# Prologue of a two-branch encoder layer: whole rows of norm weights, one scaling instruction per tile, two parameter queues, and the Newton step of four tiles on GpSimd

## Chip, cores and metric

One core of a Trainium2 chip runs the kernel. The metric is the device time of one execution in microseconds (us); lower is better. Matmul and weight load run on TensorE (PE in the profile), elementwise work on VectorE (DVE), activations and copies on ScalarE (ACT), further elementwise work on GpSimd (POOL); SP issues most of the loads.

## What is computed

```python
x = concat(x_prompt (1024 rows), x_sample (64 rows))        # 1088 x 2048, float32
h = x * rsqrt(mean(x*x, axis=-1) + EPS) * g                  # g = norm_gain, 2048
u, z_ssm, q, k, v, z_att, f = split(h @ w_in)                # 2048 x 6152
# S5 branch: dt = exp(log_dt); abar = exp(a_re*dt) * (cos(a_im*dt), sin(a_im*dt))
y_ssm, state = s5_scan(u, ...);  y_ssm = rmsnorm(glu(gelu(y_ssm)) * silu(z_ssm))
# attention branch: per-head rmsnorm of q, k; causal attention with forget gates
y_att = rmsnorm(attention(q, k, v, logf) * silu(z_att))
y = x + concat(y_ssm, y_att) @ w_out
```

One layer, float32 in and out. The prompt rows begin a stream; the 64 sample rows continue one with 128 cached rows. The outputs are y, the new cache rows and the final S5 states.

## The kernel before

**The whole.** Each float32 operand is split into a high part (rounded to the matmul's float32r type) and a low part (the remainder), and a product is three matmuls: high by high, high by low, low by high. The normalised input, transposed to features by tokens, stays on chip in two arrays, `XH` and `XL`. A prologue builds them; then come eight turns of the S5 branch (`body` of `state_space`), the attention heads, and the output projection. Nothing of the prologue runs again.

**The prologue.** It takes x in nine tiles (`TT` = 9; 128 rows each, the last has 64). For tile m:

- SP loads it (`ld_x[m]`). Tiles 2, 3 and 6 land in columns of `XHF`/`XLF` that are not yet in use (`side`), the others in two buffers `xt`; from tile 4 on a load waits until TensorE has transposed the tile that held the place (`X_FREE`). The two halves of the norm weights come, broadcast to 128 partitions, by two loads in pieces of 64 elements.
- ACT squares it and sums the row (L489, `sq_done`), then takes a square root (L491, `sqrt_done`): `x_square`.
- DVE does `x_scale`: it adds EPS (L654), takes the reciprocal of the root (L656), improves it by one Newton step of three instructions (L658 to L660), and scales the tile by that and by the norm weights in two instructions of 1024 elements a row (L665, `xs_done`).
- TensorE transposes the 16 blocks of 128 columns into four PSUM banks (`tiles`, L1030, `x_t`); it may write bank b once DVE has finished with bank b of the tile before (`x_lo`).
- ACT copies each bank to `XH` (`x_split`, L497, `x_hi`); DVE subtracts it from the bank and writes `XL` (`x_rest`, L673, `x_lo`).

Every engine runs its own instruction stream in the order in which it is written, and waits at semaphores. DVE's order is `x_scale(m + 1)`, then `x_rest(m)`, and after m = 1, 2, 3 some extra work: the low part of the gate weights (L692), of four pieces of weights (L183) and a reciprocal (L697), and for m = 3 six instructions that reduce the angles of the S5 parameters to one turn (L701 to L706, `trg_in`) and then the low part of the first tile's other weights (L709, `W.lo`). ACT's order is `x_square(m + 1)`, then `x_split(m)`; after m = 4 it takes the sine and cosine of the angles (`trg_sin`).

TensorE works between the tiles on the first column tile of the input projection (`first_tile`), on the gates (`gate`) and on two sets of transposes (`turn_c`): `first_tile(0, 0)` after tile 3, `first_tile(0, 1)` after tile 4 (it needs L709), and from tile 5 on one of them after every tile.

**The S5 parameters.** Eleven small loads on ACT's queue (`ld_par`) bring the step sizes, the poles, the states and six vectors. DVE spreads the step sizes (L678, `dt_bc`), TensorE transposes all (L1017, L1019, `par_t`), and DVE copies the result out, after `x_scale(0)`, in two instructions (L684, L685, `par_ev`). From there GpSimd evaluates two exponentials of 32 elements a row by a polynomial (`exp_poly`, L864 to L877; the first for `dtt`, the second for `mag`), forms the angles between them (L888, `arg_done`), waits for sine and cosine, builds the parameter table `pk` (L901 to L945, `pk_done`) and stores it. DVE waits for `pk_done` after `x_rest(8)`, copies the first part to `PJ` (L823), and prepares the first turn of the main loop; the last of that is the low part of the loop's first weights (L183), which TensorE waits for.

## Time and profile before

| | us |
|---|---|
| median of 3 runs | 1929.55 (1928.91 to 1931.5) |
| the profiled execution, its own time | 1928.19 |
| its span in the trace | 1926.6 |
| TensorE busy in the span | 1896.8 (98%) |
| DVE / ACT / GpSimd busy | 1137.6 / 709.2 / 441.0 |
| TensorE busy in the first 50 us of the span | 26.1 |
| chain that ended last, share on TensorE | 94% |

The 1.6 us between the profiled execution's time and its span lie around the span. The times in the trace count from the span's start. The page's rows of slices show TensorE at five tenths in the first of 40 slices (48 us each) and at nine in all others, so the prologue is the one stretch in which it stands idle for long. A row of the timeline is one instruction (or several alike, merged): its start, its duration, and in brackets the idle time of its engine just before it and what ended that.

### The profile page before, as it was taken

The page shows a single profiled execution, that of the slowest core. Times are in us where ns is not written, and L with a number is a line of the kernel's source. Part 1 is how long each engine was busy: PE and PEld are TensorE (multiplying, and loading weights), DVE is VectorE, ACT ScalarE, POOL GpSimd, SP SyncE. Part 2 cuts the span into 40 slices and gives each one's busy share as a digit, 9 for nine tenths or more (in the row PEclk, how much of TensorE's full clock was granted, in tenths as well). Part 3 has the DMA queues.
Part 4 walks back from the last instruction along what each step waited for, and adds up shares of the span by engine and source line. Part 5 has one row for each costly group of instructions (what it writes and reads, how often), then busy time and mean ns, then how long its engine had stood idle before and what let it go on. Part 6 is the DMA issues. An engine that isn't in the chain of part 4 may idle for free.

```text
span 1926.6 us, 32969 instructions
## 1 busy us (share of the span) xinstructions
PE 1896.8 (98%) x11368; PEld 1773.8 (92%) x11368; DVE 1137.6 (59%) x2189; ACT 709.2 (37%) x1395; POOL 441.0 (23%) x756
## 2 busy tenths in 40 slices
PE   5999999999999999999999999999999999999999
PEld 4899999999999999999999999999999997888877
DVE  7865665556455564545645456455566566776664
ACT  6422333333243334333343333343345443333341
POOL 5874445556112002020020200202002010100121
PEclk9999999999999999999999999999999999999999
DMA  9343343444325224132141321423338454432573
GB/s 226 105 119 108 109 109 101 120 127 123 93 74 168 84 60 143 54 108 79 55 149 57 105 80 55 139 68 94 93 99 276 153 200 139 133 122 98 180 257 122
DMA packets 212055, 230.50 MB, mean 120 GB/s; under 512 B 33978, under 2 KB 167188, under 8 KB 210772
## 3 DMA queue, kind: packets, MB, share of 16 engines
q1 hardware_dynamic: 185392, 143.58, 26.5%
q0 software_dynamic: 21072, 74.93, 11.7%
q10 hardware_dynamic: 5524, 11.14, 1.6%
q8 instruction: 37, 0.61, 0.1%
q14 instruction: 30, 0.25, 0.0%
HBM read 166.83 MB, written 62.74 MB: 119 GB/s over the span
## 4 chain that ended last, share of the span: by engine, by line
PE 94%; DVE 4%; DMA 1%; issue 0%; ACT 0%; SPq 0%; POOL 0%; POOLq 0%; DVEq 0%; ACTq 0%
PE GB L195 61%; PE TB L2350 3%; PE TB L2482 3%; PE TB L2483 3%; PE TB L2484 3%; PE TB L2371 3%; PE GB L2482 2%; PE GB L2483 2%; PE GB L2484 2%; PE TB L2392 2%; PE TB L1137 1%; PE TB L1147 1%; PE TB L1148 1%; PE TB L2411 1%; DVE XL L673 1%; PE TB L2336 0%
## 5 line engine op out<-in xcount | busy, mean ns | idle before, releaser
L195 PE MATMUL GB<-XH,whi 128*128 128x384 f32 x2448 | 827.6, 338 | 1.0 <-ACT QR L1740 0.8
L195 PE MATMUL GB<-XH,wlo 128*128 128x384 f32 x2448 | 800.5, 327 | 0.0
L195 PE MATMUL GB<-XL,whi 128*128 128x384 f32 x2448 | 798.0, 326 | 0.0
L195 PEld LDWEIGHTS GB<-XH,whi 128*128 128x128 f32 x2448 | 459.9, 188 | 14.2 <-issue 8.9
L183 DVE TENSOR_TENSOR wlo<-wraw,whi 128x256 fp32r<-128x256 f32 x412 | 201.9, 493 | 456.4 <-ACT whi L179 451.3
L195 PEld LDWEIGHTS GB<-XL,whi 128*128 128x128 f32 x2448 | 460.2, 188 | 5.3 <-issue 3.8
L195 PEld LDWEIGHTS GB<-XH,wlo 128*128 128x128 f32 x2448 | 459.3, 188 | 0.0
L179 ACT CAST whi<-wraw 128x256 fp32r<-128x256 f32 x412 | 166.5, 405 | 644.8 <-PE GB L195 634.3
L2089 DVE RECIPROCAL SQ<-SQ 128x136 f32<-128x136 f32 x128 | 127.7, 997 | 1.4
L1787 ACT ACTIVATE PR<-PR,nmx 128x128 f32<-128x128 f32 (+8 forms) x72 | 53.4, 742 | 184.4 <-DVE nmx L2060 171.8
L1545 POOL DMA_DIRECT2D t_s<-TS x16 | 11.7, 733 | 360.9 <-DVE TS L1978 311.7
L1556 POOL DMA_DIRECT2D ya_s<-ZR x7 | 4.0, 572 | 328.7 <-DVE ZR L2042 281.9
L1694 ACT CAST AREAR<-AREA 128x512 fp32r<-128x512 f32 x64 | 39.4, 621 | 98.9 <-DMA AREA<-t_s 59.1
L2350 PE MATMUL TB<-PT,VT 128*128 128x128 f32 x576 | 75.2, 276 | 0.0
L2371 PE MATMUL TB<-KN,QN 128*128 128x512 f32 (+2 forms) x192 | 72.6, 487 | 0.0
L2350 PEld LDWEIGHTS TB<-PT,VT 128*128 128x128 f32 x576 | 71.2, 191 | 1.2 <-DVE PT L2069 0.4
L1943 DVE TENSOR_TENSOR AREAR<-AREA,AREAR 128x512 fp32r<-128x512 f32 x64 | 43.4, 688 | 42.4 <-ACT AREAR L1694 42.4
L1662 ACT ACT_TABLE_LOAD x48 | 61.6, 1283 | 0.8
L2055 DVE CUSTOM_DVE_ANT_0 PR<-TB,NCB 128x128 f32<-128x128 f32 (+3 forms) x64 | 41.0, 640 | 34.4 <-PE TB L2371 23.7
L2483 PE MATMUL TB<-AREAR,XL 128*128 128x512 f32 x153 | 59.6, 390 | 0.0
L2482 PE MATMUL TB<-AREAR,XL 128*128 128x512 f32 x153 | 59.6, 390 | 0.0
L2484 PE MATMUL TB<-AREAR,XL 128*128 128x512 f32 x153 | 59.5, 389 | 0.0
(517 smaller groups left out, 2877.2 us busy)
## 6 DMA issues: line engine op xcount, KB each, us to landing
wraw<-in_w_in SPq DMA_DIRECT2D x380, 128.0 KB, 2.2
TS<-in_w_out POOLq DMA_DIRECT2D x32, 512.0 KB, 5.6
t_s<-TS POOLq DMA_DIRECT2D x16, 1024.0 KB, 4.8
AREA<-in_w_out SPq DMA_DIRECT2D x34, 256.0 KB, 3.2
AREA<-in_x_prompt POOLq DMA_DIRECT2D x32, 256.0 KB, 4.8
AREA<-t_s SPq DMA_DIRECT2D x30, 256.0 KB, 2.7
out_y_prompt<-AREA POOLq DMA_DIRECT2D x28, 256.0 KB, 3.1
xt<-in_x_prompt SPq DMA_DIRECT2D x5, 1024.0 KB, 5.4
```

Of the source, the lines that this page charges most:

```text
L179: S.copy(whi[:, s % SPL], wraw[:, s % RAW]).then_inc(self.hi, 1)
L183: V.tensor_tensor(wlo[:, s % SPL], wraw[:, s % RAW], whi[:, s % SPL].bitcast(f32), ALU.subtract).then_inc(self.lo, 1)
L195: ins = T.matmul(group(GB if bank is None else bank, b), w[:, s % SPL, kk], x[:, k + kk, c:c + n], start=first and kk == 0 and i == 0, sto ...
L1662: o.then(S.activation(tabs[:], epsc[:], func))
L1787: S.activation(PR[0:n, 0:w], PR[0:n, 0:w], ACT.Exp, bias=nmx[0:n], accum_out=rsum[0:n]).then_inc(e["exp"], 1)
L1943: V.tensor_tensor(lo, src, hi.bitcast(f32), ALU.subtract).then_inc(f["lo"], 1)
L2089: o.then(V.reciprocal(a, a))
L2350: ins = T.matmul(O, VT[:, b], PT[:, b * P:(b + 1) * P], start=b == 0, stop=b == i)
L2371: ins = T.matmul(TB[:, c:c + cw], q, KN[:, c:c + cw], start=True, stop=True)
L2482: T.matmul(bank, ah, hi, start=first, stop=False)
L2483: T.matmul(bank, al, hi, start=False, stop=False)
L2484: ins = T.matmul(bank, ah, lo, start=False, stop=last)
```

## The change

- **Norm weights.** A buffer `gain` of 2048 elements a row of its own is filled by one load whose pieces are whole rows, in place of two loads in pieces of 64.
- **Scaling.** `x_scale` scales a tile by one instruction of 2048 elements a row, in place of two of 1024.
- **Square-root table.** ACT runs a square root on a constant ahead of the first tile's square.
- **Parameter queues.** The six vectors are loaded by GpSimd's queue (`ld_vec`), the other five loads stay on ACT's. DVE waits for the five alone, TensorE for both.
- **Newton step.** For tiles 1 to 4 DVE only takes the reciprocal (`x_root`), and GpSimd adds EPS and does the Newton step in five instructions (`x_norm`). `x_norm(1)` and `x_norm(2)` stand inside the first `exp_poly`, ahead of the constants 1/720 and 1/2; `x_norm(3)` and `x_norm(4)` at the same places of the second. `x_scale` of these tiles waits for `xn_done`.
- **Orders.** `x_root(1)` comes after the copies of the parameters, `x_root(m + 2)` after `x_scale(m + 1)`. ACT does `x_square(1)` and `x_square(2)` ahead of `x_split(0)`, `x_square(3)` and `x_square(4)` ahead of `x_split(1)` and `x_split(2)`, and from there the order of before. After m = 3 DVE does the low part of the weights (L709) ahead of the angles.
- A semaphore of the output projection (`mid`) is taken from those that are spent, with an offset in its waits, so that two new ones fit.

```diff
+            gain = sbp("gain", [P, D_MODEL])
...
-            gain = [a[:, :, 8 * P:TOK] for a in (XHF, XLF)]
...
+        ld_vec, xn_done = sem("ld_vec"), sem("xn_done")
+        NORM = (1, 2, 3, 4)
...
-                for i in range(2):
-                    sp.dma_start(gain[i], norm_gain[0:1, :].to_broadcast([P, D_MODEL]).rearrange("p (k h c) -> p h k c", k=KT, h=2)[:, i]
-                                 ).then_inc(ld_gain, 16)
+                sp.dma_start(gain[:], norm_gain[0:1, :].to_broadcast([P, D_MODEL])).then_inc(ld_gain, 16)
...
-                act.dma_start(vin[0:8], ssm_d[0].rearrange("(r g) c -> r (g c)", g=8)).then_inc(ld_par, 16)
-                act.dma_start(vin[8:16], row128(b_glu)).then_inc(ld_par, 16)
-                act.dma_start(vin[16:24], row128(ssm_out_norm)).then_inc(ld_par, 16)
-                act.dma_start(vin[24:32], row128(att_out_norm)).then_inc(ld_par, 16)
-                act.dma_start(vin[32:33], q_norm_gain).then_inc(ld_par, 16)
-                act.dma_start(vin[33:34], k_norm_gain).then_inc(ld_par, 16)
-
                 act.wait_ge(ident_done, 2)
                 o = Order(act, "act_order")
+                o.then(S.activation(tabs[:], epsc[:], ACT.Sqrt))
...
                 x_square(0)
                 for m in range(TT):
-                    if m + 1 < TT:
+                    if m == 0:
+                        x_square(1)
+                        x_square(2)
+                    elif m in (1, 2):
+                        x_square(m + 2)
+                    elif 3 < m < TT - 1:
                         x_square(m + 1)
                     x_split(m)
...
+                    if m in NORM:
+                        dve.wait_ge(xn_done, NORM.index(m) + 1)
+                    else:
+                        dve.wait_ge(sq_done, m + 1)
+                        o.then(V.tensor_scalar(v, ssq[0:n, m, 0:1], EPS, None, ALU.add))
+                        dve.wait_ge(sqrt_done, m + 1)
+                        o.then(V.reciprocal(y, t))
+
+                        o.then(V.tensor_tensor(t, y, y, ALU.mult))
+                        o.then(V.scalar_tensor_tensor(t, t, -0.5, v, ALU.mult, ALU.mult))
+                        o.then(V.scalar_tensor_tensor(y, t, 1.5, y, ALU.add, ALU.mult))
                     if m == 0:
-                        dve.wait_ge(ld_gain, 32)
-                    for b in range(2):
-                        x = x_all(m)[:, :, 64 * b:64 * (b + 1)]
-                        ins = V.scalar_tensor_tensor(x, x, y, gain[b][0:n], ALU.mult, ALU.mult)
-                    ins.then_inc(xs_done, 1)
+                        dve.wait_ge(ld_gain, 16)
+                    V.scalar_tensor_tensor(x_all(m), x_all(m), y, gain[0:n].rearrange("p (k c) -> p k c", k=KT),
+                                           ALU.mult, ALU.mult).then_inc(xs_done, 1)
...
-                dve.wait_ge(ld_par, 16 * 11)
+                dve.wait_ge(ld_par, 16 * 5)
...
+                def x_root(m):
+                    n = rows[m]
+                    dve.wait_ge(sqrt_done, m + 1)
+                    V.reciprocal(ssq[0:n, m, 5:6], ssq[0:n, m, 6:7]).then_inc(par_ev, 1)
+                x_root(1)
                 for m in range(TT):
                     if m + 1 < TT:
                         x_scale(m + 1)
+                    if m + 2 in NORM:
+                        x_root(m + 2)
                     x_rest(m)
...
                     if m == 3:
+                        for p in range(SPL):
+                            dve.wait_ge(W.hi, SPL + p + 1)
+                            V.tensor_tensor(ulo[:, p], uraw[:, p], uhi[:, p].bitcast(f32), ALU.subtract).then_inc(W.lo, 1)
                         dve.wait_ge(arg_done, 1)
                         a, t, r = as_fold(arg[:]), fold[0], fold[1]
                         o.then(V.tensor_scalar(t, a, 1.0 / (2 * math.pi), MAGIC, ALU.mult, ALU.add))
...
                         o.then(V.scalar_tensor_tensor(r, t, -1.9350051879882812e-3, r, ALU.mult, ALU.add))
                         o.then(V.scalar_tensor_tensor(r, t, -3.0199159819567e-7, r, ALU.mult, ALU.add))
                         V.tensor_scalar(r, r, -3.1415925, 3.1415925, ALU.max, ALU.min).then_inc(trg_in, 1)
-                        for p in range(SPL):
-                            dve.wait_ge(W.hi, SPL + p + 1)
-                            V.tensor_tensor(ulo[:, p], uraw[:, p], uhi[:, p].bitcast(f32), ALU.subtract).then_inc(W.lo, 1)
...
+                pool.dma_start(vin[0:8], ssm_d[0].rearrange("(r g) c -> r (g c)", g=8)).then_inc(ld_vec, 16)
+                pool.dma_start(vin[8:16], row128(b_glu)).then_inc(ld_vec, 16)
+                pool.dma_start(vin[16:24], row128(ssm_out_norm)).then_inc(ld_vec, 16)
+                pool.dma_start(vin[24:32], row128(att_out_norm)).then_inc(ld_vec, 16)
+                pool.dma_start(vin[32:33], q_norm_gain).then_inc(ld_vec, 16)
+                pool.dma_start(vin[33:34], k_norm_gain).then_inc(ld_vec, 16)
+
+                def x_norm(m):
+                    n = rows[m]
+                    v, y, t = ssq[0:n, m, 4:5], ssq[0:n, m, 5:6], ssq[0:n, m, 6:7]
+                    pool.wait_ge(sq_done, m + 1)
+                    o.then(G.tensor_scalar(v, ssq[0:n, m, 0:1], EPS, None, ALU.add))
+                    pool.wait_ge(par_ev, 3 + NORM.index(m))
+                    o.then(G.tensor_tensor(t, y, y, ALU.mult))
+                    o.then(G.tensor_tensor(t, t, v, ALU.mult))
+                    o.then(G.tensor_scalar(t, t, -0.5, 1.5, ALU.mult, ALU.add))
+                    G.tensor_tensor(y, t, y, ALU.mult).then_inc(xn_done, 1)
+
+                def exp_poly(out, x, n, at):
...
                     for c in (1.0 / 720, 1.0 / 120, 1.0 / 24, 1.0 / 6, 0.5, 1.0):
+                        if at.get(c):
+                            x_norm(at[c])
                         o.then(G.tensor_scalar(out, out, c, None, ALU.add))
                         o.then(G.tensor_tensor(out, out, r, ALU.mult))
...
-                exp_poly(dtt[:], prm[:, 2], 32)
+                exp_poly(dtt[:], prm[:, 2], 32, {1.0 / 720: 1, 0.5: 2})
...
-                exp_poly(mag[:, 0], ath[:, 0], 32)
+                exp_poly(mag[:, 0], ath[:, 0], 32, {1.0 / 720: 3, 0.5: 4})
...
-                pe.wait_ge(ld_par, 16 * 11)
+                pe.wait_ge(ld_par, 16 * 5)
+                pe.wait_ge(ld_vec, 16 * 6)
...
-                        dve.wait_ge(f["mid"], 8 + 4 * c + t + 1)
+                        dve.wait_ge(f["mid"], stands["mid"] + 8 + 4 * c + t + 1)
```

## Rows read from the trace of the kernel before

**Rows 1.** Busy time by stage: engine busy us and instruction counts, clock, DMA share, GB/s.

```profile
50.00:90.20 40.20, 40.05 (x272) 32.33 (x272) 37.66 (x62) 18.49 (x38) 35.24 (x58) 1.00 0.27 85
```

**Rows 2.** Chain of work that ended last, first 200 us: start us, us, what.

```profile
1.91 4.24 SPq L353
...
6.20 8.36 DMA xt<-in_x_prompt
...
17.86 2.52 DVE xt L665 x2
...
49.25 0.61 DVE XL L673
...
50.00 2.36 PE TB L1030 x16
...
90.22 6.20 PE GB L195 x36
```

**Rows 3.** Timeline of ScalarE (ACT): start us, us, instruction, [idle before, releaser].

```profile
6.40 1.28 ACT L489 ACT_TABLE_LOAD   x1 [6.40 <-DMA xt<-in_x_prompt]
...
9.71 1.28 ACT L491 ACT_TABLE_LOAD   x1
...
19.59 1.91 ACT L489 ACTIVATE XHF<-XHF 128x2048 f32<-128x2048 f32 x1 [0.37 <-DMA XHF<-in_x_prompt]
```

**Rows 4.** DMA issues of the first 60 us: size and us to landing.

```profile
XLF<-in_norm_gain SPq DMA_DIRECT2D x1, 512.0 KB, 9.8
```

**Rows 5.** Timeline of VectorE (DVE), first 50 us.

```profile
10.14 0.21 DVE L678 COPY pk<-pk 32x128 f32<-32x128 f32 x1 [10.14 <-DMA pk<-in_k_norm_gain]
...
12.19 1.28 DVE L665 SCALAR_TENSOR_TENSOR xt<-xt,ssq,XHF 128x1024 f32<-128x1024 f32 x1
...
14.59 0.18 DVE L684 COPY vec<-GB 128x34 f32<-128x34 f32 x1
...
29.61 1.31 DVE L665 SCALAR_TENSOR_TENSOR XLF<-XLF,ssq,XHF 128x1024 f32<-128x1024 f32 x1
...
36.14 0.09 DVE L654 TENSOR_SCALAR ssq<-ssq 128x1 f32<-128x1 f32 x1
...
37.06 1.28 DVE L665 SCALAR_TENSOR_TENSOR xt<-xt,ssq,XHF 128x1024 f32<-128x1024 f32 x1
...
44.21 0.29 DVE L706 TENSOR_SCALAR XLF<-XLF 128x256 f32<-128x256 f32 x1
```

**Rows 6.** Timeline of VectorE (DVE), 60 to 180 us.

```profile
75.61 0.36 DVE L823 COPY PJ<-pk 128x397 f32<-128x397 f32 x1
```

**Rows 7.** Timeline of GpSimd (POOL), first 150 us.

```profile
15.09 0.24 POOL L881 TENSOR_TENSOR cf<-prm 128x32 f32<-128x32 f32 x1 [12.44 <-DVE prm L685]
...
17.89 0.29 POOL L869 TENSOR_SCALAR prm<-wk 128x32 f32<-128x32 f32 x1
18.26 1.03 POOL L870 TENSOR_TENSOR wk<-prm,wk 128x32 f32<-128x32 f32 x1
19.37 1.15 POOL L871 TENSOR_SCALAR dtt<-wk 128x32 f32<-128x32 f32 x1
20.60 0.29 POOL L873 TENSOR_SCALAR dtt<-dtt 128x32 f32<-128x32 f32 x1
...
21.32 0.29 POOL L873 TENSOR_SCALAR dtt<-dtt 128x32 f32<-128x32 f32 x1
...
34.45 0.54 POOL L873 TENSOR_SCALAR mag<-mag 128x32 f32<-128x32 f32 x1
...
72.02 1.29 POOL L945 TENSOR_TENSOR pk<-wk 128x512 f32<-128x512 f32 x1
...
86.07 0.21 POOL L984 TENSOR_TENSOR TR<-M 128x4 f32<-128x4 f32 x1
86.35 0.20 POOL L985 TENSOR_TENSOR M<-TR,PJ 128x4 f32<-128x4 f32 x1
```

**Rows 8.** Timeline of GpSimd (POOL), one load that it issues in the second phase.

```profile
606.67 0.58 POOL L1571 DMA_DIRECT2D CV<-in_cache_v  x1
```

More of the change, by code:

```diff
@@ L467, in scalar @@
             def scalar(act):
-                def row128(a):
-                    return a.rearrange("o (r p) -> (o r) p", p=P)
                 act.dma_start(ldt, ssm_log_dt[0].rearrange("(r g) -> r g", g=2)).then_inc(ld_par, 16)
@@ L652, in x_scale @@
                     v, y, t = ssq[0:n, m, 4:5], ssq[0:n, m, 5:6], ssq[0:n, m, 6:7]
-                    dve.wait_ge(sq_done, m + 1)
-                    o.then(V.tensor_scalar(v, ssq[0:n, m, 0:1], EPS, None, ALU.add))
-                    dve.wait_ge(sqrt_done, m + 1)
-                    o.then(V.reciprocal(y, t))
-                    o.then(V.tensor_tensor(t, y, y, ALU.mult))
-                    o.then(V.scalar_tensor_tensor(t, t, -0.5, v, ALU.mult, ALU.mult))
-                    o.then(V.scalar_tensor_tensor(y, t, 1.5, y, ALU.add, ALU.mult))
-                    if m == 0:
-                        dve.wait_ge(ld_gain, 32)
-                    for b in range(2):
-                        x = x_all(m)[:, :, 64 * b:64 * (b + 1)]
-                        ins = V.scalar_tensor_tensor(x, x, y, gain[b][0:n], ALU.mult, ALU.mult)
-                    ins.then_inc(xs_done, 1)
+                    if m in NORM:
[8 more added lines that the diff above has]
+                        o.then(V.scalar_tensor_tensor(y, t, 1.5, y, ALU.add, ALU.mult))
+                    if m == 0:
+                        dve.wait_ge(ld_gain, 16)
+                    V.scalar_tensor_tensor(x_all(m), x_all(m), y, gain[0:n].rearrange("p (k c) -> p k c", k=KT),
+                                           ALU.mult, ALU.mult).then_inc(xs_done, 1)
                 def x_rest(m):
@@ L859, in gpsimd, with row128 @@
                                 pattern=[[-1, P]], channel_multiplier=1).then_inc(ident_done, 2)
-                def exp_poly(out, x, n):
+                def row128(a):
+                    return a.rearrange("o (r p) -> (o r) p", p=P)
+                pool.dma_start(vin[0:8], ssm_d[0].rearrange("(r g) c -> r (g c)", g=8)).then_inc(ld_vec, 16)
[15 more added lines that the diff above has]
+                def exp_poly(out, x, n, at):
                     t, r = wk[:, 0, 0:n], wk[:, 1, 0:n]
@@ L1201, in attention @@
             e = {n: sem("att_" + n) for n in names}
-            spent = [(ld_gain, 32), (ld_u, 16), (ld_par, 16 * 11), (ld_b, 16 * 4), (ld_c, 16 * 16), (ld_wf, 16), (ld_x[TT - 1], 16), (gate_out, 48),
-                     (ident_done, 2), (par_t, 1), (par_ev, 2), (dt_bc, 1), (sq_done, TT), (xs_done, TT), (x_t, 4 * TT),
+            spent = [(xn_done, len(NORM)), (ld_gain, 16), (ld_u, 16), (ld_par, 16 * 5), (ld_b, 16 * 4), (ld_c, 16 * 16), (ld_wf, 16), (ld_x[TT - 1], 16), (gate_out, 48),
+                     (ident_done, 2), (par_t, 1), (par_ev, 2 + len(NORM)), (dt_bc, 1), (sq_done, TT), (xs_done, TT), (x_t, 4 * TT),
                      (x_hi, 4 * TT), (x_lo, 4 * TT), (arg_done, 1), (trg_abs, 1), (sqrt_done, TT), (trg_in, 1),
@@ L1227, in attention @@
             onames = ("ahi", "alo", "shi", "slo", "mix", "u_copy", "ss", "ms", "rt", "rs", "hi", "lo", "freed", "acc", "tmp",
-                      "ev", "r_mm")
+                      "ev", "r_mm", "mid")
             f = {n: free_sem(n) for n in onames}
-            f.update((n, sem("out_" + n)) for n in ("x_in0", "x_in1", "o_out0", "o_out1", "end_out", "mid", "fin", "r_copy"))
+            f.update((n, sem("out_" + n)) for n in ("x_in0", "x_in1", "o_out0", "o_out1", "end_out", "fin", "r_copy"))
             stands["r_copy"] = 0
@@ L2182, in join @@
                     if g // 2 == 4:
-                        dve.wait_ge(f["mid"], 4 * (g % 2) + t + 1)
+                        dve.wait_ge(f["mid"], stands["mid"] + 4 * (g % 2) + t + 1)
                         V.tensor_tensor(BX[0][:, t], BX[0][:, t], VV[g % 2][:, t], ALU.add).then_inc(f["fin"], 1)
```

## The prediction

> **What bounds the kernel now.** I read three things: the busy time by stage, to find where an edit of the prologue can count; then the chain of waits, to see which engine sets the time there; then the timelines of the three engines that the change touches. From 50.0 to 90.2 us TensorE is busy 40.05 of 40.20 us [rows 1], and after that it hardly rests. So whatever happens before 50 us counts only by one number: the time at which TensorE gets its transposes of tile 5, at 50.00. The chain says who gives them: the last piece before it is DVE's `x_rest` at L673, 49.25 to 49.86 [rows 2]. Back from there the chain stays on DVE as far as tile 1's scaling at 17.86 [rows 2], that is DVE works through 32 us without a pause. The reader should see that DVE is the bound up to 50 us, TensorE behind it, and that GpSimd, which is about to be given work, is not on the chain at all. That is the question of this change: it takes little from the engine that is the bound, and makes that engine wait for another which runs at its own pace.
>
> A second chain runs beside it. DVE hands over the angles at 44.21 + 0.29 = 44.5 us [rows 5]; ACT, then GpSimd, take them on, and GpSimd's last instruction for `pk_done` ends at 72.02 + 1.29 = 73.3 [rows 7]. DVE takes `PJ` at 75.61 [rows 6], after `x_rest(8)`, so this chain has 2.3 us to spare. From `PJ` DVE prepares the first turn until TensorE starts it at 90.22 [rows 2], and TensorE itself is full until 90.2. Both would have to come earlier to gain, and the later of them counts.
>
> **The change, part by part. Tile 0 and the start of GpSimd's work.** ACT loads a table twice around the first square, 1.28 us each, at 6.40 (when x has landed) and at 9.71 [rows 3]. With the root's table loaded during the wait for x, and the square running under it, as the rows after the second load have it (no load at 19.59 [rows 3]), both go: 2.56 us. Two scalings take 14.59 - 12.19 = 2.40 us [rows 5], 1.20 each. One of twice the length drops one fixed part; I estimate 0.13 (1.20 less 1024 elements at the row's own pace leaves at most about that), at most 0.3, at least nothing. So `x_scale(0)` ends 2.7 us earlier, at 11.9.
>
> It can be held up by two loads. The weights: before, the second half landed at 1.91 + 9.8 = 11.7 [rows 2, 4], in small pieces, and the 1 MB of tile 1 behind it at 6.20 + 8.36 = 14.56 [rows 2], 2.9 us later. x's first tile lands at 6.4 [rows 3], so 1 MB of whole rows behind it should land near 6.4 + 2.9 = 9.3; the scaling is ready for it at 12.19 - 2.56 = 9.6. If whole rows were no faster, 11.7 would cost 2.1. The vectors: the last of eleven parameters landed at 10.14 [rows 5]. GpSimd pays 0.58 an issue [rows 8], six are 3.5 us, during which it did nothing before (12.44 us idle ahead of 15.09 [rows 7]); TensorE needs them about a microsecond ahead of 11.9. I take this as free, with up to 1.5 us if the queue is slow. So GpSimd, which began on the parameters at 15.09, begins at 15.09 - 2.7 = 12.4.
>
> **Where the Newton step now stands.** This is the term that decides. Before, GpSimd went from 15.09 to the constant 1/720 of the second polynomial, at 34.45 [rows 7]: 19.4 us. DVE does tile 3's scaling at 29.61 [rows 5]. So the place at which `x_norm(3)` is written lies 5 us behind the moment at which DVE uses its result, before anything is added. Now the corrections:
>
> - DVE's scalings hold GpSimd up. During the pair for tile 1 (17.86 to 20.38 [rows 2]) three instructions of GpSimd go from 17.89 to 20.60 [rows 7]; undisturbed ones take 0.36 each (two in 21.32 - 20.60 [rows 7]). The pair cost 2.71 - 3 x 0.36 = 1.6 us. Three pairs (tiles 1, 2, 3) lay in the 19.4 us, which leaves 19.4 - 4.8 = 14.6 of work. With one long instruction no instruction of GpSimd slips in at the middle, which the one at 18.26 to 19.29 and the next at 19.37 show as the pair's seam; I put it 0.36 higher, 2.0, between 1.6 and the whole instruction, 2.3. Two lie ahead of `x_norm(3)`, for its own scaling waits for it: 4.0.
> - Three `x_norm` lie in it, of five instructions each with one element a row. The nearest rows are four elements a row, 86.35 - 86.07 = 0.28 from one to the next [rows 7]; 0.36 is the row for 32 elements. Five make 1.4 to 1.8; below, 0.20 each makes 1.0. I take 1.4.
>
> Sum: 12.4 + 14.6 + 4.0 + 3 x 1.4 = 35.2 us for the end of `x_norm(3)`, and DVE scales tile 3 at 35.3 in place of 29.61: 5.7 later. By the Trainium skill's page "SBUF — State Buffer", section "SBUF: two separate sides", a DVE instruction with two inputs in SBUF and a GpSimd instruction that reads SBUF exclude one another for the whole instruction. The three rows of tile 1 agree with it; with 2.3 for each of the two scalings the sum would be 35.8.
>
> Tiles 1 and 2 don't matter beside that. `x_norm(1)` comes at 12.4 + (20.60 - 15.09) - 1.6 = 16.3 and ends at 17.7, DVE scales where it did before (17.86); `x_norm(2)` ends at about 24 and DVE, which needs it from 23, waits a microsecond. These waits are inside GpSimd's sum. The changed order on ACT puts `x_square(2)` ahead of `x_split(0)`; it started at 19.59 with the old loads [rows 3], and even so the split would be through before DVE's second scaling has its factor.
>
> **From tile 3 to tile 5.** Tile 4's five small instructions took 37.06 - 36.14 = 0.92 [rows 5] and go, a reciprocal of 0.2 stays. From tile 3's scaling to tile 4's DVE needs 36.14 - 29.61 - 0.1 + 0.2 = 6.6 us; GpSimd needs eight instructions, 2.9, one scaling, 2.0, and an `x_norm`, 1.4, together 6.3, so `x_norm(4)` is just in time, by 0.3. If it isn't, the rest adds to the sum. Three scalings up to tile 5 save 0.13 each. So TensorE gets tile 5 later by 5.7 - 0.92 + 0.2 - 0.4 = 4.6 us. The new order of L709 lets TensorE run `first_tile(0, 1)` sooner, but TensorE then waits for tile 5 anyway: nothing. From tile 5 on the rows of before repeat, and all 40 us of TensorE move by 4.6.
>
> **The second chain.** The angles come behind L709 (four instructions, about 1.45 us) and behind a DVE that is 4.7 late at this place: 6.1 later. GpSimd's end moves from 73.3 to 79.4, and three long scalings with 0.36 more each bring it to 80.5. DVE would be free for `PJ` at 75.6 + 4.6 = 80.2. GpSimd is last by 0.3: total 4.9. Undisturbed scalings would take this back to 4.6, so I use 4.8 for the end. The six DMA issues, the semaphores of the output projection and the rest of the kernel cost nothing: 1836 us behind the prologue keep their order and start together later.
>
> The sum against the profiled execution: 1928.19 + 4.8 = 1933.0. That execution is 1.36 below the median of the runs shown, so in the measure of the medians 1929.55 + 4.8 = 1934.35, say 1934.3. A change of 0.2% is 3.9 us, about what a measurement of this kernel tells from none.
>
> **Rivals.**
>
> 1. *The same wait, but small.* `x_norm` at 1.0, a scaling's hold at 1.6: 3 x 0.4 + 2 x 0.4 = 2.0 less, and no second chain: +2.5 to +3.9, 1932.1 to 1933.4, inside 0.2%. For it speaks that an instruction of one element may be the shortest of all; against it, that every correction must fall on one side.
> 2. *GpSimd starts late.* The vectors or the weights land late (1.5 to 2.1 us), and then GpSimd's whole sum moves: +6.5 to +8, 1936 to 1937.5. For it: several queues share the loads of the first 10 us. Against: 1 us and 0.3 us of slack, worked out above.
> 3. *Faster.* GpSimd keeps up. Tile 1 has landed 2 us earlier, four Newton steps (4 x 0.75) and five scalings (5 x 0.13) leave DVE: 5.7 us less, 1923.9. It decides at one point: tile 3's scaling would have to start before 35.3 - 4.6 = 30.7. GpSimd starts at 12.4 at the earliest and has 14.6 us of undisturbed work, which makes 27.0; two holds and three Newton steps would have to fit into the 3.7 us that are left, where the rows say 8.2. I see hardly a way.
> 4. *Something hides it.* TensorE would have to have slack after 50 us; rows 1 leave 0.15 us. Only a change of pace behind the prologue would do it: within 2.5 us of before.
> 5. *Longer holds.* Each hold is the whole scaling, 2.3 us, before `x_norm(3)`, in the run-up to `x_norm(4)` and in the second chain: 4.8 + 2 x 0.3 + 0.2 + 3 x 0.3 = +6.5, 1936.0. For it speaks that 1.6 was seen only where a seam lay in the middle; against it, that the instruction at 17.89 began after the scaling and wasn't held. This is what the rule of the Trainium skill's page "SBUF — State Buffer", named above, would give.
>
> **Chances.** The forecast, +3.9 to +6.0: 0.34. Rival 5: 0.13. Rival 1: 0.26. Rival 2: 0.14. Rival 4: 0.09. Rival 3: 0.04. Slower by over 0.2%: 0.34 + 0.13 + 0.14 = 0.61; within 0.2%: 0.26 + 0.09 = 0.35; faster: 0.04. The range takes in rival 1 and nearly all of rival 2: +2.3 to +8, with a little for the medians' own spread below, 1931.6 to 1937.5.
>
> **What would show it.** In the profile of the changed kernel: no table load at ACT's first square when x lands; GpSimd's L881-instruction at 12.4; DVE idle for some 5 us ahead of tile 3's scaling, released by GpSimd, and that scaling at about 35; hardly any idle ahead of tile 4's; TensorE's tile 5 at about 54.6; the first matmul of the main loop at 95.0. If the scaling of tile 3 begins by 30, the account of GpSimd is wrong; if it is at 35 and the loop starts where it did, the account of TensorE is.

## The result and the profile after

| | before | changed |
|---|---|---|
| median of 6 runs each | 1929.39 us | 1938.30 us |
| lowest and highest | 1927.99, 1931.50 | 1935.63, 1939.60 |
| profiled execution (its span) | 1928.19 (1926.6) | 1938.14 (1936.6) |
| main loop starts in the profile | 90.22 | 96.76 |

The changed kernel is slower: the ratio is 1.0045, 95% interval 1.0035 to 1.0054, which is 8.9 us where 4.8 were predicted. The median, 1938.30, lies 0.8 us above the range. The direction and the place in the prologue were forecast, the size was not.

First the stages. The view is the busy time by stage: from and to, length, busy us and instruction counts of TensorE, its weight loads, DVE, ACT and GpSimd, then the granted clock, the DMA share and GB/s, as in [rows 1]. The two lines cover the prologue up to tile 5's transposes, and from there to the main loop.

```profile
0.00:56.50 56.50, 26.28 (x134) 24.64 (x134) 32.59 (x58) 32.00 (x54) 34.46 (x98) 0.79 0.75 208
56.50:96.80 40.30, 40.10 (x273) 32.41 (x273) 34.93 (x59) 18.58 (x38) 36.30 (x61) 1.00 0.27 84
```

The second line is [rows 1] again: TensorE is busy for 40.10 of 40.30 us. The 40 us behind tile 5 have only moved, by 6.5. So the question is what makes tile 5 late, and the chain of waits that ended last says it (start us, us, what):

```profile
3.30 6.97 DMA pk<-in_state_ssm_im
...
11.65 2.35 DVE xt L663
...
19.72 2.48 POOL dtt L901
...
26.41 2.17 POOL dtt L902
...
37.09 2.47 POOL mag L901
...
43.89 2.35 DVE xt L663
...
81.32 5.66 DMA pk_s<-pk
...
96.76 6.20 PE GB L195 x36
```

Before, this stretch of the chain was DVE from 17.86 on [rows 2]. Now it begins with a parameter load, and GpSimd stands in it. DVE's timeline shows the waits:

```profile
10.29 0.21 DVE L676 COPY pk<-pk 32x128 f32<-32x128 f32 x1 [10.29 <-DMA pk<-in_state_ssm_im]
...
11.65 2.35 DVE L663 SCALAR_TENSOR_TENSOR xt<-xt,ssq,gain 128x2048 f32<-128x2048 f32 x1
...
19.67 2.35 DVE L663 SCALAR_TENSOR_TENSOR xt<-xt,ssq,gain 128x2048 f32<-128x2048 f32 x1 [4.60 <-POOL ssq L885]
...
26.11 2.35 DVE L663 SCALAR_TENSOR_TENSOR XHF<-XHF,ssq,gain 128x2048 f32<-128x2048 f32 x1 [1.63 <-POOL ssq L885]
...
37.05 2.35 DVE L663 SCALAR_TENSOR_TENSOR XLF<-XLF,ssq,gain 128x2048 f32<-128x2048 f32 x1 [5.93 <-POOL ssq L885]
...
43.89 2.35 DVE L663 SCALAR_TENSOR_TENSOR xt<-xt,ssq,gain 128x2048 f32<-128x2048 f32 x1 [0.38 <-POOL ssq L885]
...
82.15 0.36 DVE L829 COPY PJ<-pk 128x397 f32<-128x397 f32 x1
```

The reader should see two things. DVE idles 4.60 + 1.63 + 5.93 + 0.38 = 12.5 us for GpSimd's L885, the last instruction of `x_norm`, ahead of the four scalings whose Newton step has moved. And it does nothing at all before 10.29, when the last of the five loads on ACT's queue lands. Tile 3's scaling is at 37.05 where [rows 5] had 29.61, 7.4 later. On GpSimd the same stretch reads:

```profile
14.42 0.24 POOL L909 TENSOR_TENSOR cf<-prm 128x32 f32<-128x32 f32 x1 [8.22 <-DVE prm L683]
...
18.31 0.23 POOL L880 TENSOR_SCALAR ssq<-ssq 128x1 f32<-128x1 f32 x1
18.62 0.19 POOL L882 TENSOR_TENSOR ssq<-ssq 128x1 f32<-128x1 f32 x1
...
19.45 0.19 POOL L885 TENSOR_TENSOR ssq<-ssq 128x1 f32<-128x1 f32 x1
19.72 2.47 POOL L901 TENSOR_SCALAR dtt<-dtt 128x32 f32<-128x32 f32 x1
...
26.41 2.16 POOL L902 TENSOR_TENSOR dtt<-dtt,wk 128x32 f32<-128x32 f32 x1
...
36.82 0.19 POOL L885 TENSOR_TENSOR ssq<-ssq 128x1 f32<-128x1 f32 x1
```

From the first line to the last GpSimd rests nowhere; that takes 22.6 us, and DVE's scaling of tile 3 can't start before it.

TensorE gets tile 5 at 56.54 in place of 50.00 [rows 2], then all is as before until far behind the prologue. The two spans differ by 10.0 us: 6.54 by the loop's start, 0.76 from there to the second of two groups of sums of squares at the start of the output projection, 1.57 in the stretch behind that group, 1.13 after it. For the 1.57 the stages of the two executions:

```profile
1585.00:1599.00 14.00, 14.00 (x72) 11.45 (x71) 6.39 (x16) 2.69 (x5) 0.00 (x0) 0.88 0.40 151
```

```profile
1592.00:1607.00 15.00, 15.00 (x72) 12.39 (x71) 6.68 (x16) 2.83 (x5) 0.00 (x0) 0.77 0.36 135
```

The first is before, the second the changed kernel: 72 matmuls in 14 and in 15 us, TensorE busy throughout, its granted clock at 0.88 and 0.77 of full speed. That is, in the second it was longer at the lower of its two levels, 1.2 GHz. The timeline shows where: each group of sums of squares is 20 matmuls of one column, and behind such a group matmuls of 512 columns take 0.63 us in place of 0.39 for a while. In the kernel before this follows the first group alone, in the changed kernel both. The same place behind the second group, before and changed:

```profile
1594.67 0.39 PE L2484 MATMUL GB<-AREAR,XL 128*128 128x512 f32 x1
```

```profile
1602.28 0.63 PE L2513 MATMUL GB<-AREAR,XL 128*128 128x512 f32 x1
```

The sum had nothing for this; the experiments ask whether it belongs to the change.

### The profile page after: what moved, and what is told of

The parts are those of the page before. It is cut to its first block, busy times and chain, and to the rows that moved or that the text cites. A ratio compares the mean times of both kernels' runs of the same rounds, so it can differ in the third digit from the quotient of the medians.

```text
span 1936.6 us, 32968 instructions
## 1 busy us (share of the span) xinstructions
PE 1898.8 (98%) x11368; PEld 1775.5 (92%) x11368; DVE 1130.7 (58%) x2164; ACT 707.5 (37%) x1395; POOL 449.9 (23%) x782
## 4 chain that ended last, share of the span: by engine, by line
PE 87%; DVE 5%; DMA 3%; POOL 3%; issue 1%; ACT 1%; ACTq 0%; POOLq 0%; SPq 0%; DVEq 0%
PE GB L195 59%; PE TB L2379 3%; PE TB L2400 3%; PE TB L2511 3%; PE TB L2513 3%; PE TB L2512 3%; PE GB L2511 2%; PE GB L2512 2%; PE TB L2421 2%; PE GB L2513 2%; PE TB L1166 1%; PE TB L1176 1%; PE TB L1177 1%; PE TB L2440 1%; PE TB L2365 0%
```

## The experiments

I held this theory, T: the loss is GpSimd's single stream. `x_norm(3)` stands behind all of GpSimd's earlier work, and that work starts 2 us later than predicted because DVE's first instruction waits for the five loads. Its rivals: the delay is nothing by itself and something else of the change costs it (the new order on ACT and DVE, the two queues, a semaphore that the output projection now counts differently); and what lies behind the prologue is its own effect. The table holds what the runs gave, "kernel before" being the median of the runs beside it; the edits and what follows are below. The ratio is taken over the runs and isn't the quotient of the two medians. The two kernels without an interval have one execution each. The kernel before scales tile 3 at 29.61 [rows 5] and starts the loop at 90.22 [rows 2].

| run | median | kernel before | ratio, 95% | tile 3 scaled | loop starts |
|---|---|---|---|---|---|
| the change | 1938.30 | 1929.39 | 1.0045 [1.0035, 1.0054] | 37.05 | 96.76 |
| e1 | 1932.34 | 1929.57 | 1.0017 [1.0008, 1.0026] | 29.93 | 92.57 |
| e2 | 1933.09 | 1929.57 | 1.0017 [1.0007, 1.0026] | 31.95 | 92.76 |
| e3 | 1930.45 | 1929.57 | 1.0005 [0.9996, 1.0014] | 29.38 | 89.97 |
| e4 | 1936.58 | 1929.57 | 1.0034 [1.0021, 1.0047] | 36.24 | 96.66 |
| e5 | 1929.44 | 1929.24 | 1.0002 [0.9993, 1.0011] | 27.59 | 88.78 |
| e6 | 1934.95 | 1929.24 | | 37.65 | 97.39 |
| e7 | 1937.04 | 1929.24 | | 36.71 | 96.40 |
| e8 | 1935.87 | 1929.24 | 1.0036 [1.0022, 1.0049] | 36.20 | 96.31 |
| e9 | 1936.94 | 1929.42 | 1.0033 [1.0020, 1.0046] | 37.20 | 96.93 |
| e10 | 1930.09 | 1929.42 | 1.0004 [0.9995, 1.0012] | 30.15 | 90.73 |
| e11 | 1930.38 | 1929.42 | 1.0004 [0.9995, 1.0013] | 30.13 | 90.36 |

**e1: the changed kernel with the Newton step on DVE.**

```diff
-        NORM = (1, 2, 3, 4)
+        NORM = ()
...
-                x_root(1)
...
-                exp_poly(dtt[:], prm[:, 2], 32, {1.0 / 720: 1, 0.5: 2})
+                exp_poly(dtt[:], prm[:, 2], 32, {})
...
-                exp_poly(mag[:, 0], ath[:, 0], 32, {1.0 / 720: 3, 0.5: 4})
+                exp_poly(mag[:, 0], ath[:, 0], 32, {})
```

> The changed kernel with no tile's Newton step on GpSimd: DVE does the five small instructions for every tile, all else as changed (whole rows, one scaling, two queues, table load, ACT's order). Theory A (DVE waits for GpSimd, and that is the prologue's loss): the 4.6, 1.6 and 5.9 us of idle on DVE ahead of tiles 1, 2 and 3 go; what is left is the late start (parameters land at 10.3 us) and ACT's order, which puts tile 4's square, whose load lands at 30.9, ahead of the split of tile 2. I work out tile 5's transposes at 51.7 us (50.0 before, 56.5 changed) and the main loop at 92 (90.2 and 96.8). Theory B (the late start of everything is the loss, GpSimd only fills the wait): the main loop stays within 1 us of 96.8. Total by A: 4 to 5 us under the changed kernel; what is above 2 us over the kernel before then sits in the output projection.

It gives back 4.2 of the 6.5 us of the loop's start. Tile 3 is scaled at 29.93, within 0.3 us of before the change. In the measured time it is 2.8 us above the kernel before in place of 8.9, that is 6.1 less where I had expected 4 to 5. Two waits are left on DVE, and they are for ACT:

```profile
20.56 2.48 DVE L671 TENSOR_TENSOR XL<-TB,XH 128x512 fp32r<-128x512 f32 x4 [2.47 <-ACT XH L489]
...
33.58 2.48 DVE L671 TENSOR_TENSOR XL<-TB,XH 128x512 fp32r<-128x512 f32 x4 [1.27 <-ACT XH L489]
```

ACT's new order puts two squares ahead of the first split. With the Newton step on GpSimd that wait is hidden under the wait for GpSimd; without it, it shows. So the moved step carries the larger part, and the order of ACT is a loss of its own that lay under it.

At tile 5 more comes back than at the loop's start, 5.6 us:

```profile
50.91 2.82 PE L1058 MATMUL TB<-ident,xt 128*128 128x128 f32 x16 [2.43 <-DVE XL L671]
```

```profile
50.91:92.57 41.66, 41.49 (x272) 33.39 (x273) 36.07 (x59) 18.51 (x38) 36.25 (x60) 0.96 0.25 81
```

From tile 5 to the loop TensorE took 40.2 us before and takes 41.7 here, busy throughout, at a granted clock of 0.96 over the stretch (0.68 in its first 4 us). Of the 2.35 us by which e1's loop starts later than before, 1.4 are thus TensorE's clock and 0.9 the prologue on DVE.

**e2: the Newton step stays on GpSimd, but earlier.** `x_norm(3)` comes right behind the first polynomial, `x_norm(4)` ahead of the second.

```diff
                 exp_poly(dtt[:], prm[:, 2], 32, {1.0 / 720: 1, 0.5: 2})
+                x_norm(3)
...
+                x_norm(4)
-                exp_poly(mag[:, 0], ath[:, 0], 32, {1.0 / 720: 3, 0.5: 4})
+                exp_poly(mag[:, 0], ath[:, 0], 32, {})
```

> The changed kernel with two of the GpSimd steps written earlier: x_norm(3) right behind the first polynomial, x_norm(4) ahead of the second one, in place of ahead of 1/720 and 1/2 in the second. By theory A (the place in GpSimd's stream decides) x_norm(3) ends at about 31.8 us in place of 37.0, DVE's scaling of tile 3 starts at 31.9, that of tile 4 at 38.4 (43.9 changed, 37.1 before), and the main loop at about 91.2 in place of 96.8. By theory C (GpSimd is slow because it is held up, wherever the step is written) tile 3's scaling comes within 2 us of 37.0.

The first line is GpSimd's, the next two are DVE's, the last two TensorE's:

```profile
31.73 0.19 POOL L885 TENSOR_TENSOR ssq<-ssq 128x1 f32<-128x1 f32 x1
```

```profile
31.95 2.39 DVE L663 SCALAR_TENSOR_TENSOR XLF<-XLF,ssq,gain 128x2048 f32<-128x2048 f32 x1 [0.64 <-POOL ssq L885]
...
84.06 1.15 DVE L737 TENSOR_TENSOR UC<-PJ 128x576 f32<-128x576 f32 x1 [1.51 <-DMA pk_s<-pk]
```

```profile
50.86 2.96 PE L1061 MATMUL TB<-ident,xt 128*128 128x128 f32 x16 [2.08 <-DVE XL L671]
...
92.76 0.44 PE L195 MATMUL GB<-XH,whi 128*128 128x384 f32 x1 [0.38 <-DVE wlo L183]
```

The same five instructions in another place of the same stream, and the 5.93 us of waiting ahead of tile 3 are 0.64. This shows that it was the place in the stream. Tile 5 comes at 50.86, 5.7 earlier than in the changed kernel, and yet the loop's start comes back by 4.0 and not by the 5.6 expected. Most of what is missing is TensorE's clock, as in e1: it is busy for 41.52 us between tile 5 and the loop, where before it was 40.05, at a granted clock of 0.96. The second chain adds little. It holds DVE up for 1.51 until the store of `pk` has landed, but TensorE, which is full meanwhile, waits for DVE only 0.38 at the loop's start, where it waits 0.17 in the changed kernel: 0.2 us.

**e3: the kernel before with the semaphore of the change alone** ("mid" counts on from where it stands, as the changed kernel has it):

```diff
-                        dve.wait_ge(f["mid"], 8 + 4 * c + t + 1)
+                        dve.wait_ge(f["mid"], stands["mid"] + 8 + 4 * c + t + 1)
```

> The kernel before with only the semaphore of the output projection changed as in the change (taken from those spent, waits with an offset). In the changed kernel's trace 3.4 of the 10 us lie behind the prologue: 2.4 at the start of the output projection, where TensorE has a granted clock of 0.7 to 0.8 in some 15 us where before it was below full speed in 5, and 1 us at the end. Theory S (the semaphore's new waits do it): this kernel is 2 to 3.5 us slower than before. Theory P (the clock falls at a point that depends on when the stretch is reached, and the semaphore does nothing): same within 0.5 us, but for the chance of the clock.

No difference from before can be told; by the interval up to 2.7 us isn't excluded.

**e4: the kernel before with a delay.** Three memsets of 1.76 us ahead of tile 3's scaling, and nothing else.

```diff
+            idle = sbp("idle", [P, D_MODEL])
...
+                    if m == 3:
+                        for i in range(3):
+                            o.then(V.memset(idle[:], 0.0))
```

> The kernel before with three memsets of a buffer of its own, 2048 elements a row, on DVE ahead of tile 3's scaling: some 6.5 us of nothing on the engine that sets the prologue's time. Main loop later by 6.5 (at 96.7), as in the changed kernel, with nothing else changed. Theory P (a later arrival alone changes the clock's course in the output projection): the total grows by 8 to 10 us. Theory S (only the change's own code does it): by 6.5.

```profile
29.93 1.76 DVE L666 MEMSET idle<- 128x2048 f32 x1 [0.49 <-DVE ssq L661]
32.19 1.76 DVE L666 MEMSET idle<- 128x2048 f32 x1 [0.49 <-DVE idle L666]
34.44 1.76 DVE L666 MEMSET idle<- 128x2048 f32 x1 [0.49 <-DVE idle L666]
36.24 1.28 DVE L669 SCALAR_TENSOR_TENSOR XLF<-XLF,ssq,XHF 128x1024 f32<-128x1024 f32 x1
```

This is the kernel before in everything but 6.6 us of DVE's time at this place, and the loop starts 6.4 later, the end comes 7.0 later. By the medians a delay at tile 3 goes through to the end one for one, without anything else of the change (by the interval 4.1 to 9.1 us). It also has the longer stretch behind the second group of sums of squares: from that group to the next step it takes 7.11 us as against 5.52 before and 7.09 in the changed kernel.

**e8: e4 and e3 together.**

> The kernel before with both the 6.5 us of memsets of e4_delay_before and the semaphore of e3_semaphore_only. The changed kernel was 8.9 us above the kernel before with the main loop 6.5 late; e4 was 7.0 above (6.6 by the ratio) with the same start, e3 0.9 (1.0). Theory S (the semaphore's waits cost about 1 to 2 us): this one is 8 to 9 us above. Theory P (the rest is the course of the clock and the spread of the runs): 6.5 to 7.5.

No difference from e4 can be told, so nothing here speaks for the semaphore; the interval is as wide as e4's.

**e5: e1, and ACT in the order of before.** What is left of the change is the whole rows of weights, the one scaling a tile, the table load moved ahead, the two queues, the semaphore and the order of L709.

```diff
-                    if m == 0:
-                        x_square(1)
-                        x_square(2)
-                    elif m in (1, 2):
-                        x_square(m + 2)
-                    elif 3 < m < TT - 1:
+                    if m + 1 < TT:
                         x_square(m + 1)
```

> As e1_newton_dve (no Newton step on GpSimd), and ACT in the order of the kernel before: one square ahead of each split. In e1 DVE still waited 2.5 us for tile 0's split, which stood behind the square of tile 2 (its load lands at 18.05), and 1.3 us for tile 2's split, behind the square of tile 4 (load at 30.9). Theory A: both waits go, tile 5's transposes come 2 to 3 us ahead of the kernel before (at 47 to 48), the main loop starts at about 87.5 to 88.5, and the total is 1.5 to 3 us under the kernel before. Theory B (the prologue cannot come earlier than before, another chain holds it): the main loop at 90 or later. The second chain (angles, GpSimd, table) is the one that could.

The waits for ACT at tiles 0 and 2 are gone, and TensorE has tile 5 at 47.59, 2.4 us ahead of [rows 2]. The loop starts only 1.4 ahead, and here is the rest:

```profile
47.59 3.37 PE L1053 MATMUL TB<-ident,xt 128*128 128x128 f32 x16 [3.02 <-DVE XL L666]
```

```profile
47.60:52.00 4.40, 4.40 (x25) 4.07 (x26) 2.44 (x8) 4.37 (x7) 3.89 (x13) 0.66 0.25 104
```

The sixteen transposes that take 2.36 us in [rows 2] take 3.37: TensorE had been idle for 3.02 us ahead of them, and they run at a granted clock of 0.66. I had expected the total 1.5 to 3 us under the kernel before and missed: in the measured time e5 can't be told from it, so the 1.4 us are shown in the profile alone.

**e6 and e7: what makes GpSimd start at 14.42.** e6 is the changed kernel with the weights loaded in two halves, in the pieces of before; e7 is the changed kernel with tile 0's scaling ahead of the parameters' copies.

```diff
-                sp.dma_start(gain[:], norm_gain[0:1, :].to_broadcast([P, D_MODEL])).then_inc(ld_gain, 16)
+                for i in range(2):
+                    sp.dma_start(gain[:].rearrange("p (k h c) -> p h k c", k=KT, h=2)[:, i],
...
```

```diff
+                x_scale(0)
                 dve.wait_ge(ld_par, 16 * 5)
...
-                x_scale(0)
```

> The changed kernel with the norm weights loaded by two loads in pieces of 64 elements, as before, into the new buffer. In the changed kernel the last of the five parameter loads on ACT's queue landed at 10.29, 7.0 us after its issue, though it had six loads fewer behind it than before. Theory Q (whole rows of 8 KB ahead of them in the same DMA engines hold the small loads up): they land by 8.5 here, and the weights later, at 11 to 12. Theory T (these loads take that long whatever runs beside): they land at 10 to 10.5 again.

> The changed kernel with DVE doing tile 0 ahead of the two instructions that wait for the five parameter loads. Theory A: tile 0's scaling starts at 9.7 (weights landed at 9.4) in place of 11.65, but the parameters are spread, transposed and copied behind it, so GpSimd starts at 13.7 in place of 14.42, x_norm(3) ends at 36.3 in place of 37.0, and the main loop comes 0.7 earlier, at 96.0. If GpSimd's start were not the bound, the loop would stay at 96.8.

DVE in e6, then in e7:

```profile
9.62 0.22 DVE L679 COPY pk<-pk 32x128 f32<-32x128 f32 x1 [9.62 <-DMA pk<-in_state_ssm_im]
...
12.20 2.35 DVE L666 SCALAR_TENSOR_TENSOR xt<-xt,ssq,gain 128x2048 f32<-128x2048 f32 x1 [1.25 <-DMA gain<-in_norm_gain]
```

```profile
9.71 2.35 DVE L663 SCALAR_TENSOR_TENSOR xt<-xt,ssq,gain 128x2048 f32<-128x2048 f32 x1
...
13.58 0.19 DVE L682 COPY vec<-GB 128x34 f32<-128x34 f32 x1 [1.11 <-PE GB L1048]
```

Both kernels have one execution each, so their profiles are read and their times are not compared. In e6 the five loads land 0.67 us earlier than in the changed kernel, which is between what the two theories expected, and the weights are then what tile 0 waits for: in pieces they come 2.5 us later than tile 0 could be scaled in e7. In e7 tile 0's scaling stands at 9.71, where my prediction had it (9.6), and the whole rows had landed by then. But the parameters are now behind it, GpSimd begins at 14.09 and tile 3 is scaled at 36.71. So neither order on DVE gives GpSimd its start at 12.4, and in e7 DVE waits 1.11 us for TensorE's transposes of the parameters. What TensorE waits for, in the kernel before, the changed kernel, e7 and e6:

```profile
10.50 0.29 PE L1017 MATMUL GB<-ident,pk 34*128 34x34 f32 x1 [10.50 <-DVE pk L678]
```

```profile
12.72 0.29 PE L1046 MATMUL GB<-ident,pk 34*128 34x34 f32 x1 [12.72 <-DMA pk<-in_k_norm_gain]
```

```profile
12.59 0.29 PE L1046 MATMUL GB<-ident,pk 34*128 34x34 f32 x1 [12.59 <-DMA pk<-in_k_norm_gain]
```

```profile
10.87 0.29 PE L1049 MATMUL GB<-ident,pk 34*128 34x34 f32 x1 [10.87 <-DMA pk<-in_k_norm_gain]
```

In the last three it is the last of the six vectors on GpSimd's queue. TensorE has it at about 12.7 beside the whole rows and at 10.87 beside the pieces. So a second cause of the same size stands beside the five loads. In the changed kernel TensorE is through at 13.67 and the copies wait for tile 0's scaling until 13.92, so the vectors are hidden; in e7, where the scaling is early, they alone set GpSimd's start to 14.09. T named only the first of the two. A kernel with both out of the way and the weights still early wasn't run.

**e9: the changed kernel again.**

> The changed kernel once more, to tell how much of the part behind the prologue is a property of the kernel. Its 8.9 us were 6.5 of main loop start and 2.4 behind it; the two kernels with the delay alone were 6.6 to 7.0 above for the same start. If the 2.4 belong to the kernel, it is 8.5 to 9.5 above again; if they are the spread of the runs, 6.5 to 8.

By the medians it is 7.5 us slower than before in place of 8.9, with the loop at 96.93; by the intervals of the ratios, 3.9 to 8.9 us here and 6.8 to 10.4 in the first measurement. So one and the same kernel, taken against the kernel before, moves by 1.4 us between two measurements.

**e10: the kernel before with the two queues** (vectors on GpSimd's queue, five loads on ACT's), and **e11: e5 with all eleven loads on ACT's queue.**

```diff
-                act.dma_start(vin[0:8], ssm_d[0].rearrange("(r g) c -> r (g c)", g=8)).then_inc(ld_par, 16)
...
+                pool.dma_start(vin[0:8], ssm_d[0].rearrange("(r g) c -> r (g c)", g=8)).then_inc(ld_vec, 16)
```

> The kernel before with the six vectors on GpSimd's queue (and the semaphore of e3, which makes room for the second one), nothing else. DVE still waits for the five loads on ACT's queue; e6 had them at 9.62 with the weights in pieces, before had all eleven at 10.14. So DVE begins at 9.6 to 10.1, tile 0's scaling is bound by ACT's root at 11.3 anyway, and the main loop starts within 0.3 us of 90.2. If GpSimd's six additional loads cost something behind the prologue (all kernels with them were 1 to 2 us above what their main loop start explains), the total is 1 to 2 us above the kernel before; if not, it is the same.

> As e5_act_order, with all eleven parameter loads on ACT's queue, as before. If the five loads land late because of what runs beside them and not because of the queue, the last of eleven now lands at 10.5 to 11.5, ACT's table load moves from 4.0 to 6.1 and the first square from 6.5 to 7.6; tile 0's scaling starts by 12.5, tile 1's by 16 (its load lands at 12.4), and the main loop at 88.8, as in e5. If GpSimd's loads cost 1 to 2 us behind the prologue, the total falls to 1 to 2 us under the kernel before; if not, it stays within 0.5 us of e5.

DVE's first instruction in e10, then in e11:

```profile
9.63 0.21 DVE L670 COPY pk<-pk 32x128 f32<-32x128 f32 x1 [9.63 <-DMA pk<-in_state_ssm_im]
```

```profile
12.83 0.22 DVE L679 COPY pk<-pk 32x128 f32<-32x128 f32 x1 [12.83 <-DMA pk<-in_k_norm_gain]
```

With weights in pieces, five loads land at 9.63 and all eleven at 10.14 [rows 5]: the second queue brings 0.5. With whole rows, five land at 10.37 (e5) and eleven at 12.83: there the second queue brings 2.5. Without it tile 5 comes 2.5 later than in e5 and the loop starts 1.6 later, since e11 doesn't have e5's lower clock at tile 5 (its transposes take 2.36). I had expected 10.5 to 11.5 and missed: I had taken the slow-down for the same in both, and beside whole rows eleven small loads lose 2.7 us where five lose 0.7. By the profile the whole rows thus need the second queue, which in the kernel before (e10) brings nothing; in the measured time neither e10 nor e11 can be told from before, so neither shows a cost of GpSimd's loads behind the prologue.

## Why the prediction was right in kind and too small

The measured 8.9 us are 4.1 more than the 4.8 predicted: 1.7 of these are in the loop's start and come in the main from step 2, 2.4 lie behind it (step 7). By the prediction's own steps, with what the changed kernel's profile and the runs say:

1. **The bound.** Right. Up to tile 5 only DVE's order counted, and TensorE was full behind it (40.10 of 40.30 us). e4 shows it directly: 6.6 us put in at tile 3 are 6.4 at the loop and 7.0 at the end. That the 40.2 us from tile 5 to the loop stay the same held for the changed kernel, but not in e1, e2 and e5 (41.7, 41.9 and 41.2).
2. **Tile 0 and GpSimd's start at 12.4. This step failed.** It was 14.42, 2.0 later. The two table loads went, as said, the single scaling saved 0.13 (13.92 - 11.65 = 2.27 in place of 2.40), as said, and the weights in whole rows were there for 9.71 (e7), as said. The five parameter loads had no term, though DVE's first instruction, which stands ahead of tile 0's scaling, waits for them. I had read the 10.14 of [rows 5] with the name of the releaser, the last of eleven loads, and took the six vectors in front of it for what made it late. But the wait was for the whole queue; the five that stayed landed at 10.29, no sooner than all eleven before, since the whole rows beside them slow them (9.62 in e6). So tile 0's scaling came at 11.65 in place of 9.6. The vectors, taken as free, were not free either: TensorE was to have them about a microsecond ahead of 11.9 and began at 12.72. Beside the five loads this cost nothing more, but alone it would have made the start 14.1 (e7). Rival 2 had this outcome at the loop's start, +6.5 to +8, and named the vectors; it didn't name the five loads, which ended last here, and it got 0.14.
3. **GpSimd's sum.** Right: predicted 14.6 + 4.0 + 4.2 = 22.8 from start to the end of `x_norm(3)`, measured 37.01 - 14.42 = 22.6. `x_norm` takes 1.41 (from 18.31 to 19.72, where 1.4 was taken). The two held instructions cost 2.47 - 0.29 = 2.2 and 2.16 - 0.25 = 1.9, where 2.0 was taken. Both end within 0.2 us of the scaling during which they run (19.67 + 2.35 = 22.02, and 19.72 + 2.47 = 22.19). This agrees with the rule of the Trainium skill's page "SBUF — State Buffer", section "SBUF: two separate sides", by which one of the two waits until the other's whole instruction is done; what it costs is a little less than the 2.35, since the held instruction's own time is in it and the second one began 0.3 after the scaling. Of the three rows of tile 1, which the prediction called in agreement with the rule, the first doesn't show it: it began 0.03 after the scaling and took 0.29, unheld. With starts so close the rows don't say which came first. Rival 5, whose sum of +6.5 is also that of the loop's start, isn't what happened: its holds of 2.3 would have made 0.3 more each, and step 2's 2.0 us weren't in it.
4. **Tile 3.** Predicted 35.3 and found at 37.05, 1.75 later, which is step 2's 2.0 less step 3's 0.2, to within 0.1. e2 shows that the place in the stream is the cause: the same instructions earlier, and the wait falls from 5.93 to 0.64.
5. **Tile 4 just in time.** By a hair not: DVE waited 0.38. Tile 5 came 6.5 later (predicted 4.6).
6. **The second chain, +0.2.** Wrong and small: `pk_done` came at 81.0, 1.1 before DVE took `PJ` at 82.15, so it added nothing there. Its store held DVE for 0.23, and TensorE's wait at the loop's start is 0.17 as before. In e2, where DVE is earlier, the store holds it for 1.5, of which 0.2 reach TensorE.
7. **What lies behind the prologue, nothing.** Here 8.9 - 6.5 = 2.4 us are outside the prologue and outside the sum. In the profiled executions the time from the loop's start to the end of the span is 1836.4 in the kernel before, 1839.8 and 1839.0 in the two of the changed kernel, and between 1836.0 and 1839.9 in the others, with e10 (hardly changed) at the top and e6 (nearly the changed kernel) at the bottom. In the output projection the two stretches behind the groups of sums of squares take either 5.5 or 7.1 us each, by the granted clock, in no order that follows the edits: 7.1 and 5.5 in the kernel before, 7.1 and 7.1 in the changed kernel, but 5.5 and 7.1 in its second execution (e9), as much in sum as before; twice 5.5 in e6, twice 7.1 in e4. So the 1.57 us of the first comparison are not a property of the change. The last 330 us spread by 3 us as well, from 329.0 (e4, e8) to 332.0 (e9). Executions of the kernel before spread over 7 us by themselves (1926.08 to 1933.22 beside e9). e9 brought the 2.4 down to 0.8 (7.5 less its own 6.7 at the loop's start) without a change. So most of it is spread of the executions. That up to a microsecond or two belongs to the change isn't excluded, and what decides whether the clock falls behind such a group is open.

The sum with step 2 as measured is 4.8 + 2.0 = +6.8, 1936.3 in the measure of the prediction, inside its range and within e9's interval, and at the lower end of the first measurement's.

What was lost, then, is shown: e1 takes the Newton step away and 4.2 us come back (5.6 at tile 5); e5 takes ACT's order away too and another 3.8 come with it (3.3 at tile 5), to a loop start 1.4 us ahead of before. The gain of the whole rows, the single scaling and the earlier table is there in the profile, but 1 us of it falls to TensorE's clock at tile 5, and the end can't tell what remains (1.0002, 0.9993 to 1.0011). How it divides among the three wasn't tested. No version measured faster than the kernel before.

## What to carry to other kernels

Work that is moved off the bounding engine onto an idle-looking one costs its place in that engine's stream: add up what stands ahead of it, from the start that it will really have, and compare with the moment at which the result is used. Where an instruction waits for a whole queue of loads, the profile names the one that came last; price the others as well before you take that one away, beside the transfers that the change itself makes larger, and price the loads that you moved on their new queue. Removing one of two causes of the same size shows little: e7 took the first away and found the second.

## What the runs showed of the hardware

- A GpSimd elementwise instruction that began during one of DVE's 2.35 us scalings was held to its end: 2.47 and 2.16 us in place of 0.29 and 0.25, in the changed kernel at each of tiles 1 to 4, twice ahead of `x_norm(3)`. Where GpSimd holds up DVE, that price falls on DVE again.
- A Newton step of five instructions of one element a row is 1.4 us on GpSimd, 0.28 from one to the next; on DVE the five of the kernel before take 0.92 [rows 5].
- The loads of 0.5 to 16 KB took 5.6 to 7.2 us to land during the first 10 us, and their end depended on the form of a transfer on another queue. Eleven of them had landed at 10.14 beside the weights in pieces (two loads of 512 KB), at 12.83 beside 1 MB in whole rows; five at 9.6 and 10.3 to 10.5; the six on GpSimd's queue at 10.9 and 12.1 to 12.7, by TensorE's wait for them. The lines are those of the DMA issues of the changed kernel, size and us to landing:

```profile
gain<-in_norm_gain SPq DMA_DIRECT2D x1, 1024.0 KB, 8.0
...
pk<-in_state_ssm_re ACTq DMA_DIRECT2D x1, 16.0 KB, 7.2
...
pk<-in_k_norm_gain POOLq DMA_DIRECT2D x1, 0.5 KB, 6.8
```

- Earlier work is not always faster work on TensorE: transposes that came 2.4 us earlier, behind 3.02 us of idleness, ran at a granted clock of 0.66 and took 3.37 in place of 2.36 us (e5). The idle time just ahead of them doesn't decide it alone: behind 2.08 (e2) and 2.43 us (e1) they took 2.96 and 2.82, behind 2.20 us (e11) 2.36.
